# Attention values as the stationary operand, two heads side by side, with one turn-back and one scaling per head pair

## What is computed

```python
def _fox_attend(q, k, v, c_q, c_k, pos_q, pos_k):
    s = jnp.einsum('bqhd,bkhd->bhqk', q, k).astype(jnp.float32) * (HD_B ** -0.5)
    s = s + (jnp.swapaxes(c_q, 1, 2)[..., :, None] - jnp.swapaxes(c_k, 1, 2)[..., None, :])
    s = jnp.where((pos_k[None, :] <= pos_q[:, None])[None, None], s, -jnp.inf)
    p = jax.nn.softmax(s, axis=-1).astype(v.dtype)
    return jnp.einsum('bhqk,bkhd->bqhd', p, v)
# dsa: the same with one key and one value head shared by four query heads,
# over the 256 keys that an indexer chose for each query (a penalty of -1e30 on the others)
```

## Time and profile before

| | us |
|---|---|
| median of 3 runs | 2413.16 |
| the profiled execution | 2415.18 |
| its span, first to last instruction | 2413.4 |
| TensorE busy | 2159.6 (89%) |
| VectorE busy | 1446.0 (60%) |
| ScalarE busy | 649.2 (27%) |
| mean granted TensorE clock, of full speed | 0.931 |

### The profile page before, as it was taken

One profiled execution on the slowest core, in us unless ns is written; L12 is line 12 of the kernel. 1 busy time (PEld: TensorE's weight loads), 2 busy tenths in 40 slices (PEclk: granted clock), 3 DMA queues, 4 the chain that ended last, 5 costly groups with the idle time before them and its releaser, 6 DMA issues. The chain is left out here.

```text
span 2413.4 us, 27568 instructions
## 1 busy us (share of the span) xinstructions
PE 2159.6 (89%) x10002; PEld 1290.9 (53%) x10002; DVE 1446.0 (60%) x3157; ACT 649.2 (27%) x1486; POOL 259.7 (11%) x364
## 2 busy tenths in 40 slices
PE   4999876789998999999969998768899989999998
PEld 3534445544445776764444344555444457777643
DVE  3368588888944754541134677888899267444321
ACT  3351323321102223321144503323311122333211
POOL 0000333321000000001100004233210000000011
PEclk9999987899997789999979999879999967899999
DMA  8101220213213002213341111212132120022143
GB/s 286 56 26 69 81 85 29 75 44 116 83 38 71 12 5 84 73 44 132 131 172 53 59 62 54 81 41 75 50 106 83 42 58 14 3 86 71 44 157 124
DMA packets 151110, 179.39 MB, mean 74 GB/s; under 512 B 71312, under 2 KB 106640, under 8 KB 150704
## 3 DMA queue, kind: packets, MB, share of 16 engines
q1 hardware_dynamic: 122912, 140.23, 18.4%
q10 hardware_dynamic: 28064, 37.38, 4.4%
HBM read 120.25 MB, written 67.22 MB: 78 GB/s over the span
## 5 line engine op out<-in xcount | busy, mean ns | idle before, releaser
L822 PE MATMUL ps<-wring,xnT_arena 128*128 128x512 f32 (+2 forms) x2304 | 933.2, 549 | 0.0
L822 PEld LDWEIGHTS ps<-wring,xnT_arena 128*128 128x128 f32 x2304 | 424.3, 197 | 383.7 <-issue 365.4
L1562 DVE TENSOR_SCALAR_CACHE_REDUCE arena<-arena,theta 32x1056 bf16<-32x1056 f32 x496 | 458.9, 978 | 2.2
L1159 PE MATMUL ps<-wring,arena 128*128 128x512 f32 x576 | 251.8, 596 | 0.0
L1775 DVE TENSOR_REDUCE small<-ps 128x1 f32<-128x192 f32 (+9 forms) x148 | 114.1, 771 | 142.9 <-PE ps L1093 140.7
L1159 PEld LDWEIGHTS ps<-wring,arena 128*128 128x128 f32 x576 | 109.2, 192 | 131.2 <-issue 131.2
L1459 ACT ACTIVATE arena<-ps,small 128x192 f32<-128x192 f32 (+9 forms) x148 | 111.0, 750 | 215.9 <-DVE small L1775 215.5
L1091 PE MATMUL ps<-xnT_arena,arena 128*128 128x64 f32 (+4 forms) x336 | 123.5, 500 | 20.0 <-DVE xnT_arena L1201 18.9
L1237 ACT COPY arena<-ps 128x512 f32<-128x512 f32 (+2 forms) x108 | 55.1, 510 | 313.0 <-PE ps L822 287.2
L958 PE MATMUL ps<-arena 128*128 128x128 f32 x488 | 90.1, 313 | 45.8 <-DVE arena L1667 45.6
L1130 PE MATMUL ps<-xnT_arena 128*128 128x64 f32 (+1 forms) x720 | 126.7, 324 | 0.7 <-issue 0.7
(11 more groups left out here) (241 smaller groups left out, 2555.6 us busy)
## 6 DMA issues: line engine op xcount, KB each, us to landing
projected<-arena ACTq DMA_DIRECT2D x130, 256.0 KB, 2.0
wring<-in_w_in SPq DMA_DIRECT2D x16, 1024.0 KB, 8.2
arena<-residual SPq DMA_DIRECT2D x30, 512.0 KB, 4.9
o_bc<-projected SPq DMA_DIRECT2D x36, 384.0 KB, 3.6
wring<-in_w_in SPq DMA_DIRECT2D x6, 2048.0 KB, 8.8
arena<-projected SPq DMA_DIRECT2D x18, 512.0 KB, 5.2
residual<-arena SPq DMA_DIRECT2D x18, 512.0 KB, 2.6
wring<-in_w_out SPq DMA_DIRECT2D x8, 1024.0 KB, 6.0
```

The lines of the kernel that those rows point to most:

```text
L822: o = mm(bank(pbank(k), 0, w_), xnT[:, c, t * P:(t + 1) * P], w, start=(c == 0), stop=(c == CH - 1))
L1159: o = mm(bank(4 - 4 * (t % 2) + half), yT[t % 2][:, c, :], wring[:, c * D + 512 * half:c * D + 512 * half + 512], start=(c == 0), stop=(c ...
L1562: V.tensor_scalar(cmp_out[r, (i % 2) * WMAX:(i % 2) * WMAX + uw[u]], score[u][r], th_, 0.0, op, ALU.add, accum_out=into[r, i:i + 1]).then_ ...
```

## The change

The values become the stationary operand (64 columns) and the turned probabilities move (128 columns). Two heads of one unit are multiplied in turn, the even one into partitions 0 to 63 of bank 7, the odd one into 64 to 127. The result, (two heads x 64) by 128 queries, is copied to SBUF by ScalarE (`oTs`), turned back by one transposition into columns 128 to 255 of bank 7 (`turn_back`), and scaled by VectorE in one instruction for both heads. "pv" is now an entry per head pair, `PV`, and "back" a new kind of entry. A pair's "pv" comes where its second head's did, and "back" behind the next "turn", or right ahead of the next "pv" where no turn stands between (for unit 8, and for a last head ahead of unit 8, the values follow right behind the job's own turn). Written out for units 3 and 7 the order becomes: score L1, turn S1, score S2, turn L1, exp S2, **pv S(0,1)**, score L2, turn S2, **back S(0,1)**, exp L2, **pv L(0,1)**, score S3, turn L2, **back L(0,1)**, exp S3, score L3, turn S3, exp L3, turn L3. Four `ptile` buffers take the place of two, and the sums have eight slots.

```diff
+        ptile = [ca([NT * P]) for _ in range(2)] + [sb(f"ptile{i}", [P, 4 * P])[:, :] for i in range(2)]
+        oTs = [ca([P]) for _ in range(2)]
...
                 seq.append(("turn", job))
+                seq += [("back", p) for p in PV[-1:] if p[1] != "s" and ("back", p) not in seq]
...
-                if n > 0:
-                    seq.append(("pv", AJ[n - 1]))
-            return seq + [("pv", AJ[-1])]
+                single = lambda i: len(UNIT_GROUPS[i % len(UNIT_GROUPS)]) == 1
+                ready = AJ[max(0, n - 1):n] + ([job] if single(g[1]) or (job == mine[-1] and single(g[1] + 1)) else [])
+                for m, u, h in ready:
+                    if (u == "s" or h % 2) and (m, u, h // 2) not in PV:
+                        seq += [("back", p) for p in PV[-1:] if p[1] != "s" and ("back", p) not in seq]
+                        PV.append((m, u, h // 2))
+                        seq.append(("pv", PV[-1]))
+            return seq + [("back", PV[-1])]
...
+                    def values(m, u, hp_):
+                        i = pv_no[m, u, hp_]
+                        for h in ([0] if u == "s" else [2 * hp_, 2 * hp_ + 1]):
+                            turned((m, u, h))
+                        if i >= 1:
+                            pe.wait_ge(a_o, a_o_at[PV[i - 1]])
...
-                                v = foxV[0:w, i, h * HD:(h + 1) * HD] if m == "fox" else dsaKV[0:w, i, HD:2 * HD]
-                                o = mm(ps[:, o0:o0 + HD], pt, v, start=(i == 0), stop=(i == len(ch) - 1), skip_group_check=True)
+                            order = list(range(1, len(ch))) + [0]
+                            for c in order:
+                                w = ch[c][1]
+                                for e in range(2):
+                                    h = 2 * hp_ + e
+                                    v = foxV[0:w, c, h * HD:(h + 1) * HD] if m == "fox" else dsaKV[0:w, c, HD:2 * HD]
+                                    o = mm(ps[HD * e:HD * e + HD, o0:o0 + P], v, ptile[pt_of[m, u, h]][0:w, P * c:P * c + P],
+                                           start=(c == order[0]), stop=(c == order[-1]), skip_group_check=True)
                         o.then_inc(a_pv, 1)
+                    def turn_back(m, u, hp_):
+                        i = pv_no[m, u, hp_]
+                        pe.wait_ge(a_ot, a_ot_at[m, u, hp_])
+                        tr(ps[:, 7 * 512 + P:7 * 512 + 2 * P], oTs[i % 2], C("ident")).then_inc(a_back, 1)
...
(ScalarE, in its walk through PLAN)
+                        elif what == "pv" and key[1] != "s":
+                            i = pv_no[key]
+                            act.wait_ge(a_pv, a_pv_at[key])
+                            if i >= 2 and PV[i - 2][1] != "s":
+                                act.wait_ge(a_back, a_back_at[PV[i - 2]])
+                            nc.scalar.copy(oTs[i % 2], ps[:, 7 * 512:7 * 512 + P]).then_inc(a_ot, 1)
...
(VectorE, in finish)
-                            o = V.tensor_scalar(o_bc[r, u, c0 + HD * h:c0 + HD * h + HD], ps[r, o0:o0 + HD], rinv[r, n % 4:n % 4 + 1], None, ALU.mult)
-                            o.then_inc(a_o, 1)
+                            V.reciprocal(rinv[:, s:s + 2], rsum[:, s:s + 2]).then_inc(dve_own, one_more(own))
+                            dve.wait_ge(dve_own, own[0])
+                            dve.wait_ge(a_back, a_back_at[m, u, hp_])
                             r = slice(32, HALF) if u == 0 else slice(0, P)
+                            V.tensor_tensor(o_bc[r, u, c0 + P * hp_:c0 + P * hp_ + P].rearrange("p (e d) -> p e d", e=2),
+                                            ps[r, o0 + P:o0 + 2 * P].rearrange("p (e d) -> p e d", e=2),
+                                            rinv[r, s:s + 2][:, :, None].broadcast_to([r.stop - r.start, 2, HD]), ALU.mult).then_inc(a_o, 1)
...
-                        elif what == "pv":
+                        elif what == ("pv" if key[1] == "s" else "back"):
                             finish(*key)
```

More of the change, by code:

```diff
@@ L336, in encoder @@
         ss, rr = small[:, 0:NT], small[:, 16:16 + NT]
-        mneg, rsum = small[:, 32:36], small[:, 44:48]
+        mneg, rsum, rinv = (sb(n, [P, 8])[:, :] for n in ("mneg", "rsum", "rinv"))
         hs, hr = small[:, 56:64], small[:, 64:72]
         oss, orr, ors = small[:, 72:73], small[:, 73:74], small[:, 74:75]
-        rinv = small[:, 76:80]
         sel = sb("sel", [P, 7, 8])
@@ L485, in plan_attend @@
                     seq.append(("exp", AJ[n + 1]))
-                if n > 0:
-                    seq.append(("pv", AJ[n - 1]))
-            return seq + [("pv", AJ[-1])]
-        PLAN = plan_attend()
+                single = lambda i: len(UNIT_GROUPS[i % len(UNIT_GROUPS)]) == 1
[6 more added lines that the diff above has]
+            return seq + [("back", PV[-1])]
+        PV = []
+        PLAN = plan_attend()
+        pair = lambda job: (job[0], job[1], job[2] // 2)
+        pv_no = {p: i for i, p in enumerate(PV)}
+        slot_of = {j: 2 * (pv_no[pair(j)] % 4) + j[2] % 2 for j in AJ}
+        small_unit = lambda u: u != "s" and any(len(group) == 2 and group[0] == u for group in UNIT_GROUPS)
+        pt_of = {j: (2 if small_unit(j[1]) else 0) + j[2] % 2 for j in AJ}
+        pt_before = {j: ([i for i in AJ[:AJ.index(j)] if pt_of[i] == pt_of[j]] or [None])[-1] for j in AJ}
         job_no = {j: i for i, j in enumerate(AJ)}
@@ L506, in encoder @@
         a_exp, a_exp_at = sem("a_exp"), steps(AJ)
-        a_pv, a_pv_at = sem("a_pv"), steps(AJ)
-        a_o, a_o_at = sem("a_o"), steps(AJ)
+        a_pv, a_pv_at = sem("a_pv"), steps(PV)
+        a_ot, a_ot_at = sem("a_ot"), steps([p for p in PV if p[1] != "s"])
+        a_back, a_back_at = sem("a_back"), steps([p for p in PV if p[1] != "s"])
+        a_o, a_o_at = sem("a_o"), steps(PV)
         preps = [a for a in AT if a[0] != "p"]
@@ L1106, in turn @@
                             o.then_inc(a_tr, 1)
[L1108 to L1113, removed]
+                    def values(m, u, hp_):
[4 more added lines that the diff above has]
+                            pe.wait_ge(a_o, a_o_at[PV[i - 1]])
+                        if m == "fox" and hp_ == 0:
                             if u == "s":
@@ L1117, in values @@
                                 pe.wait_ge(ld_v, 16)
[L1118 to L1122, removed]
+                        ch = pieces_of((m, u))
+                        o0 = 7 * 512
+                        if u == "s":
+                            for c, (key, w, _) in enumerate(ch):
+                                pt = ptile[pt_of[m, u, 0]][0:w, P * c:P * c + P]
@@ L1127, in values @@
[L1127 to L1130 removed]
+                                    v = dsaVc[:, c - 1, :] if c else dsaKV[0:NS, 0, HD:2 * HD]
@@ new lines, in values @@
+                                    o = mm(ps[:, o0:o0 + HD], pt, v, start=(c == 0), stop=(c == len(ch) - 1), skip_group_check=True)
+                        else:
+                            order = list(range(1, len(ch))) + [0]
[6 more added lines that the diff above has]
+                                           start=(c == order[0]), stop=(c == order[-1]), skip_group_check=True)
@@ L1143, in _ @@
                             values(*key)
+                        elif what == "back":
+                            turn_back(*key)
                     pe.wait_ge(attend_end["A"], 1)
@@ L1200, in copy_p @@
                     size = P * len(pt_groups((m, u))[g])
-                    copy(ptile[n % 2][:, 4 * g * P:4 * g * P + size], bank(tbank[a], 0, size)).then_inc(te, 1)
+                    copy(ptile[pt_of[m, u, h]][:, 4 * g * P:4 * g * P + size], bank(tbank[a], 0, size)).then_inc(te, 1)
                 @block.scalar
@@ L1430, in turn_evac @@
                         else:
-                            if job_no[a[1:4]] >= 2:
-                                act.wait_ge(a_pv, a_pv_at[AJ[job_no[a[1:4]] - 2]])
+                            if pt_before[a[1:4]] is not None:
+                                act.wait_ge(a_pv, a_pv_at[pair(pt_before[a[1:4]])])
                             copy_p(nc.scalar.copy, a, a_teA)
@@ L1780, in _ @@
                                     dve.wait_ge(a_tr, a_tr_at[a])
+                                    if pt_before[key] is not None:
+                                        dve.wait_ge(a_pv, a_pv_at[pair(pt_before[key])])
                                     copy_p(V.tensor_copy, a, a_teD)
-                        elif what == "pv":
+                        elif what == ("pv" if key[1] == "s" else "back"):
                             finish(*key)
                     V.memset(o_bc[HALF:, 0], 0.0).then_inc(dve_own, one_more(own))
-                    dve.wait_ge(a_o, a_o_at[AJ[-1]])
+                    dve.wait_ge(a_o, a_o_at[PV[-1]])
                     dve.wait_ge(dve_own, own[0])
```

25 lines of the change are left out of this document (11 added, 14 removed).

## The result

The kernel after takes 2440.36 us, the median of six runs (2437.66 to 2445.72); the kernel before, timed beside it, takes 2420.41 (six runs, 2409.24 to 2424.99). The ratio is 1.0093, 95% interval 1.0067 to 1.0118: slower by 0.9%, some 20 us, where 15 + 55 = +70 was forecast. The profiled execution took 2445.72 us. It is the slowest of the six, and that of before (2415.18) lies 5 us under the median of its runs, so the two profiles lie 30 us apart and not 20.

The account below looks back on a forecast made before the run. The prediction took TensorE as the bound by a hair, with the large unit's softmax hidden behind the values. Profiled 2415.2 + 15 (unchanged clock) + 55 (clock falls) = 2485, so a median of 2483 us, range 2410 to 2550.

Parts of the forecast that it names:

- TensorE's own work: Attention values and turn-backs on TensorE: cheaper values save 93 us, turn-backs return 14, together 78 us less at full clock.
- the forecast's -11.9 and +7.6: Unit 8, alone in its group: values -11.9 + 7.6 and turn-backs +0.6 give -3.7 us, before added waits.
- The change of tiling: TensorE switching its tiling mode twice for every head pair: claimed to add nothing, read from the trace's start times.
- Each switch drains: Rival: each tiling switch, twice for each of 72 pairs, empties TensorE, 30 us more, 2513; chance 0.05.
- The busy round: Units 3 and 7, L's values waiting for the scaling of S's pair: 10.05 us, 1.97 more than 8.08.
- The quiet round: Units 3 and 7, none of L's values between its scores and its turn: 6.93 us, 1.15 less than 8.08.
- Dsa at an unchanged clock: The dsa half of attention, with its new waits of TensorE and unit 8: +12 us in each layer.
- Fox: Fox half, per layer: units 3, 7 and 8 +1.5 us; units 0 to 6 -6, between -14 and +12.
- The sum at an unchanged clock: Both attention halves together: 12 + 1.5 - 6 = 7.5 us per layer, +15 us in all.
- 10 falls, +55 us: Dsa and last fox units, 380 us: TensorE's clock drops to half for 16 us ten times, 5.3 us each.
- The clock holds: Rival: dsa's gaps do not lower TensorE's clock, so only the 15 us stand: 2428 to 2430; chance 0.15.

Follow-up runs that it names:

- e1: The changed kernel with the turned-back result in a bank of its own for most pairs: 2396.17 us, ratio to before 0.9903.
- e3: The changed kernel with most turned-back results in their own bank and small units' turned probabilities copied out by ScalarE: 2394.41 us, ratio to before 0.9907.
- e5: The changed kernel with one more VectorE reduction over 960 columns ahead of each dsa scaling: 2479.32 us, ratio to before 1.028.
- e6: The changed kernel with one more VectorE reduction over 1920 columns ahead of each dsa scaling: 2521.86 us, ratio to before 1.0453.

## Why the prediction was off

**TensorE's own work** (-78 us): measured -78.3 busy, which counts time at half clock too and so is no test of the sum at full clock. A pair with 8 pieces takes 2.04 (2.02 forecast), one with 4 1.17 (1.06): 0.30 + 0.22 for each piece instead of 0.1 + 0.24, so that by the rows the values save 87 us rather than 93. For unit 8 the forecast's -11.9 and +7.6 do not follow from its rows (four heads at 2.2 are 8.8, two pairs 4.5), but their sum, -4.3, does.

**The change of tiling** (nothing added). The prediction read 494.43 against 494.35 as an overlap, but the ends of matmuls are modelled; starts tell more. Eight transpositions step to the values in 0.97 us (1032.12 to 1033.09), four in 0.53: 0.11 each, and 0.09 over at the change. The weight loads (PEld) pause at each of the three changes of a pair, to column halves, to column halves of 64 rows and back to the whole array:

```profile
1033.09 0.63 PEld L1151 LDWEIGHTS ps<-ptile,arena 128*64 128x64 f32 x12 [0.17 <-issue]
1033.89 0.20 PEld L1151 LDWEIGHTS ps<-ptile,arena 64*64 64x64 f32 x4 [0.17 <-issue]
1034.26 0.30 PEld L1106 LDWEIGHTS ps<-arena 128*128 128x128 f32 x2 [0.17 <-issue]
```

The kernel before has the same pause where its transpositions end and the first piece of 64 keys begins:

```profile
1026.65 1.11 PEld L1130 LDWEIGHTS ps<-arena,xnT_arena 64*128 64x128 f32 x8 [0.17 <-issue]
```

What is not steps is 0.30 us for a pair now and was 2 x 0.18 for two heads. So nothing was added, as forecast, but because the kernel before had such changes too, not because they are free. The Trainium skill, TensorEngine Tiling (Key Properties), has the engine drain at each change of tiling mode. The pauses agree with that in kind; the 0.2 us at each change that the rival "Each switch drains" reckoned are not seen, and what a change costs, the kernel before paid too.

**The busy round** (+1.97, 10.05): 9.88. Wait for the scaling 2.50 from the scores' end (2.7 forecast), the scaling itself 0.29 (0.35 taken). e1 shows that this wait alone is worth more than the loss.

**The quiet round** (-1.15, 6.93): 7.78, only 0.30 less than 8.08. A wait was missed. The scores of S2 need the banks that VectorE empties of S1's turn, and VectorE does that behind L's maximum: they start at 1030.85, 1.41 us late, and with them the turn of L comes 3.29 us after the scores' end instead of 2.60. In e3, with that copy on ScalarE, it is 2.60.

**Dsa at an unchanged clock** (+12 per layer): in layer 2 the three stages give 7.4 + 3.0 + 5.8 and the tail gives back 2.0: +14.2. In layer 1 it is +20, of which 4.5 is the long fall (unit 8: 25.5 against 21.0). Each has one more fall of 3.4 us in it.

**Fox.** Units 3, 7 and 8, +1.5 forecast: +4.5 and +4.8. Units 0 to 6, -6 forecast between -14 and +12: -7.8 and -13.7, but not at an unchanged clock. The stretches of this stage, before in layers 1 and 2, then after in layer 2 (layer 1 is above, 0.78):

```profile
753.00:871.00 118.00, 103.69 (x508) 80.58 (x506) 84.24 (x175) 30.87 (x78) 0.81 (x5) 0.73 0.07 14
1945.00:2066.00 121.00, 108.18 (x505) 84.20 (x503) 84.06 (x174) 30.94 (x78) 0.52 (x4) 0.69 0.07 14
...
1969.00:2076.00 107.00, 82.55 (x502) 58.84 (x500) 79.16 (x150) 32.27 (x88) 0.67 (x4) 0.81 0.08 17
```

The clock rose from 0.73 to 0.78 and from 0.69 to 0.81: some 50 us less at half clock in both layers. What that is worth is read from runs of the same fox code: e5 and e6 do not touch it, and the stage takes 104.7 to 105.6 us there at clocks of 0.85 to 0.87 and 110.7 at 0.78, some 0.29 us for each at half clock. So by an estimate 14 of the 21.5 us that fox gained are the clock's, and 3 to 4 in each layer the change's own, near the 4.6 that VectorE drops.

**The sum at an unchanged clock** (+15) was therefore too low, and that the measured +20 lies near it is luck. The attention is 22 us longer; without fox's 14 from the clock and the 7 to 8 that the falls below cost, the estimate is 28 to 29. The forecast lacked some 3 us per layer in fox units 3, 7 and 8, 1 to 2 in dsa, where the quiet round's wait was missed, and 2 to 3 in fox units 0 to 6.

**The step that failed is the clock's**: "Dsa and the last fox units are 380 us in both layers: 10 falls, +55 us". Neither the count nor the length came. From 865 to 1085 and from 2076 to 2294 the mean clock is 0.96 and 0.98, that is 26 us at half clock (0.08 x 220 + 0.04 x 218), where the forecast had ten times 16. There are five falls up to the last exponentials. The windows of the kernel after, TensorE alone (length, busy, granted clock), show what they look like:

```profile
945.00:950.00 5.00, 4.28 (x18) 0.66 0.42 168
950.00:1055.00 105.00, 80.55 (x658) 1.00 0.15 43
1055.00:1070.00 15.00, 12.89 (x63) 0.66 0.00 1
```

Four are like the first row: 0.66 over 5 us, 3.4 us at 1.2 GHz. Only one lasted ten (last row). The kernel before had some 4 us at half clock in each layer of the same code, the ends of long falls from the penalty stretch. The 18 us that are new cost 7 to 8 us by an estimate: the long fall cost 4.5 us for ten, and e5's 14 us for 34 are 0.40 for each, a little over the forecast's price of 1 - 1/1.5 = 0.33. With fox's 14 us on the other side the clock as a whole did not cost 55 us but gave some 7 back; over the whole execution it rose from 0.931 to 0.937. The forecast took the length of a fall and its frequency from the penalty stretch, because the share of idle time would be the same there and in the new dsa; 105 us at 77% busy and a clock of 1.00 show that the share does not carry over. The rival "The clock holds", at 2428 to 2430, was the nearest, by the luck told above.

What stays open: why fox's clock rose, and why one fall in dsa came and its twin did not. In layer 1 it began after idle times of 2.00 and 1.66 us within 9 us; in layer 2 the same two stand at the same place, with the clock at 1.00 over the whole stretch:

```profile
2260.92 1.06 PE L1120 MATMUL ps<-cf,arena 128*64 128x128 f32 x8 [2.00 <-ACT arena L1488]
2267.33 0.33 PE L1158 MATMUL ps<-cf,xnT_arena 128*128 128x128 f32 x1 [1.66 <-ACT xnT_arena L1507]
```

Of the 8.3 us outside the attention, the clock between the two attentions (17 us more at half clock, at 0.29 some 5 us, an estimate) may be the larger part; the rest is not explained.

## What to carry to other kernels

Work that is saved on the bounding engine counts only if nothing was hidden behind it: list, for each instruction that gets shorter or moves, the chain that ran beside it, and then walk the other engines' queues entry by entry, since the two waits that decided here (a scaling behind a maximum and a copy; scores behind the same copy) both stood in VectorE's order. When a cheaper form of an operation loses, look first at the wait that ties its buffers together: a second bank for a 128x128 result was worth 44 us, more than the whole loss. And a clock that falls in one stretch is no measure for another stretch with the same idle share: price both cases, and before a stage's gain or loss is put down to the change, compare its granted clock before and after.

## What was not expected of the hardware

TensorE kept 2.4 GHz over 120 us with idle times of 1 to 2 us every few us and 77% busy, and had a mean clock of 0.80 and 0.81 over such stretches once those in busy rounds were 3 to 4 us (e6). The falls in dsa and the last fox units last 3 to 10 us, not 16. Two column halves side by side step exactly twice as fast, 0.054 against 0.108 us for each instruction, with the same operands in another order. And in the rows shown a change of tiling leaves the weight loads idle for 0.17 us, before as after.
